# Hybrid attention block on one core: where the inverse softmax sums are turned, where the values are taken, and how many choice portions a step holds

## The reference, cut to what matters

```
h    = rms_norm(x, g_in);  proj = h @ w_in        # q, k, v, gate, indexer columns
oA   = dilated-window attention, 8 heads          # pairs "A": bias table per head
oB   = attention of 4 heads over the 256 keys that an indexer scores highest
oM   = cross attention of 4 heads into 256 memory tokens
o    = concat(oA, oB, oM) * silu(gate)
out  = rms_norm(x + o @ w_out, g_final)
```

## Time and profile before

| | |
|---|---|
| median of 3 runs | 714.0 us (713.66 to 715.45) |
| the profiled execution's own time | 713.12 us |
| its span | 711.3 us |
| PE busy | 673.2 us (95%) |
| DVE busy | 421.2 us (59%) |
| ACT busy | 333.4 us (47%) |
| POOL busy | 143.4 us (20%) |
| mean granted clock of PE | 0.994 |
| steps 8 to 15 (pair 1) | 187.8 to 260.9 us |
| steps 16 to 23 (pair 2) | 260.9 to 334.4 us |
| steps 24 to 31 (pair 3) | 334.4 to 409.1 us |

### The profile page before, as it was taken

One profiled execution on the slowest core, in us unless ns is written; L12 is line 12 of the kernel. 1 busy time (PEld: TensorE's weight loads), 2 busy tenths in 40 slices (PEclk: granted clock), 3 DMA queues, 4 the chain that ended last, 5 costly groups with the idle time before them and its releaser, 6 DMA issues.

```text
span 711.3 us, 11577 instructions
## 1 busy us (share of the span) xinstructions
PE 673.2 (95%) x4281; PEld 537.5 (76%) x4281; DVE 421.2 (59%) x991; ACT 333.4 (47%) x632; POOL 143.4 (20%) x95
## 2 busy tenths in 40 slices
PE   5999999999999999999999999989999999999993
PEld 4788887777778777787777777877888777777772
DVE  4857874396788576975797685652343354122247
ACT  6876653343335342644255434653563585122223
POOL 2021110111323013113114114210111166212101
PEclk9999999999999999999999999999999999999997
DMA  8521120111311121112111311101111416410005
GB/s 296 165 60 30 30 78 13 29 30 46 89 45 34 43 90 45 29 47 89 45 31 45 88 47 31 45 2 45 45 30 43 152 53 239 158 34 23 0 30 207
DMA packets 51863, 47.71 MB, mean 67 GB/s; under 512 B 5712, under 2 KB 44640, under 8 KB 51808
## 3 DMA queue, kind: packets, MB, share of 16 engines
q1 hardware_dynamic: 51808, 46.97, 21.6%
HBM read 39.62 MB, written 7.34 MB: 66 GB/s over the span
## 4 chain that ended last, share of the span: by engine, by line
PE 81%; DVE 10%; issue 3%; ACT 3%; DMA 2%; DVEq 0%; SPq 0%; ACTq 0%
PE j_ps L1471 27%; PE s_ps L1471 9%; PE o_ps L1630 8%; PE pt_ps L1604 7%; PE s_ps L1533 6%; PE s_ps L1680 5%; PE j_ps L1680 4%; PE o_ps L1471 4%; PE s_ps L1553 3%; DVE unread L1221 2%; PE pt_ps L1553 2%; PE s_ps L1686 1%; PE pt_ps L1652 1%; PE o_ps L1447 1%; PE j_ps L1447 1%
## 5 line engine op out<-in xcount | busy, mean ns | idle before, releaser
L1471 PE MATMUL j_ps<-h_hi,w_hl 128*128 128x512 f32 (+2 forms) x656 | 213.2, 391 | 4.7 <-DVE h_lo L1080 2.8
L1471 PEld LDWEIGHTS j_ps<-h_hi,w_hl 128*128 128x128 f32 (+1 forms) x656 | 121.1, 186 | 30.5 <-issue 4.9
L713 POOL TENSOR_TENSOR w_hl<-w_raw,w_hl 128x1024 fp32r<-128x1024 f32 (+1 forms) x29 | 68.2, 2350 | 322.7 <-ACT w_hl L815 311.4
L1471 PE MATMUL j_ps<-h_lo,w_hl 128*128 128x512 f32 (+2 forms) x328 | 125.4, 382 | 0.0
L998 ACT ACTIVATE prob<-prob,nmax 128x256 f32<-128x256 f32 (+7 forms) x128 | 89.9, 704 | 68.8 <-DVE nmax L1294 56.8
L986 ACT ACTIVATE probT<-pt_ps 128x512 f32<-128x512 f32 (+3 forms) x88 | 41.2, 468 | 124.3 <-PE pt_ps L1604 123.8
L1604 PE MATMUL pt_ps<-ident,prob 128*128 128x128 f32 x496 | 72.9, 280 | 8.9 <-DVE gate L1321 4.5
L1471 PE MATMUL s_ps<-h_hi,w_hl 128*128 128x512 f32 x224 | 73.7, 397 | 0.9 <-ACT qk L859 0.9
L1604 PEld LDWEIGHTS pt_ps<-ident,prob 128*128 128x128 f32 x496 | 54.5, 140 | 25.9 <-issue 18.8
L1471 PEld LDWEIGHTS j_ps<-h_lo,w_hl 128*128 128x128 f32 (+1 forms) x328 | 61.1, 186 | 11.1
L1221 DVE TENSOR_SCALAR_CACHE_REDUCE unread<-idx,tk 128x384 uint8<-128x384 f32 (+5 forms) x72 | 67.8, 942 | 1.3
(11 more groups left out here) (246 smaller groups left out, 1062.3 us busy)
## 6 DMA issues: line engine op xcount, KB each, us to landing
w_raw<-in_w_in_dram SPq DMA_DIRECT2D x27, 512.0 KB, 4.0
idx<-in_x_dram SPq DMA_DIRECT2D x8, 512.0 KB, 6.0
bias<-in_a_tab_dram SPq DMA_DIRECT2D x8, 512.0 KB, 4.7
mixed_scratch<-gate SPq DMA_DIRECT2D x12, 256.0 KB, 2.3
bias<-in_x_dram SPq DMA_DIRECT2D x4, 512.0 KB, 6.6
probT<-in_w_mem_kv_dram SPq DMA_DIRECT2D x4, 512.0 KB, 6.7
bias<-in_w_out_dram SPq DMA_DIRECT2D x4, 512.0 KB, 4.4
out_dram<-idx SPq DMA_DIRECT2D x4, 512.0 KB, 3.3
```

What stands on the lines that cost most here:

```text
L713: pool.tensor_tensor(w_hl[:, w % 2, 1, :, 0:n], raw_of(w)[:, :, 0:n], w_hl[:, w % 2, 0, :, 0:n].bitcast(F32), ALU.subtract).then_inc(w_lo_ ...
L1471: last = pe.matmul(bank[0:n, at:], a[:, k, 0:n], c[:, k, HALF * b + at:HALF * b + HALF], start=(k == 0 and q == 0), stop=(k == KD - 1 and ...
```

## The change

It has three parts.

1. The inverse sums get a PSUM bank of their own, `sums_bank = s_ps[1][:, HALF:T]`. For the groups of pairs 0 to 5 they are turned and multiplied into the gate in the first two steps of the next pair: group (p, g) in step 8(p+1) + g. `turn_sums` stands right behind `scores` there, `even_out` behind the copies, and the inversion is made a step earlier. Group (6, 0) goes to step 57. Groups (6, 1), (7, 0) and (7, 1) are handled in the step that ends them (`AT_ONCE`: 56, 60, 64), with `turn_sums` ahead of (or between) the values. The stores to the scratch tensor and the copies for the output projection wait for `linv_used` as well. `turn_prob` and `turn_values` no longer wait for it; a wide step's scores do.
2. Outside `AT_ONCE` the product of gate and values (`take_values`) stands behind `choose_portions(s, 1)`, the last portions of its step.
3. `choice_room` of an A pair becomes (2,2) for i = 0 and (1,2) for i = 4. With it every later slot moves to an earlier step; the last tile is settled in step 32. Slots per step, before and after (n.k is slot k of tile n):

The diff, cut to its core:

```diff
-PART_AT = {STEPS - NT - 3: (NP - 2, 0), STEPS - NT: (NP - 2, 1), STEPS - 4: (NP - 1, 0), STEPS: (NP - 1, 1)}
+PART_AT = {STEPS - NT: (NP - 2, 1), STEPS - NT + 1: (NP - 2, 0), STEPS - 4: (NP - 1, 0), STEPS: (NP - 1, 1)}
+EVEN_AT = {NT * (p + 1) + g: (p, g) for p in range(NP - 2) for g in range(2)}
+EVEN_AT.update(PART_AT)
+AT_ONCE = [s for s, (p, g) in EVEN_AT.items() if s == NT * p + 4 * g + 4 and p >= NP - 2]
+def evened(p, g):
+    return EVENED.index((p, g)) + 1
@@ choice_room
-    return [(2, 1), (2, 2), (2, 2), (2, 2), (1, 1), (1, 1), (1, 1), (1, 1)][i]
+    return [(2, 2), (2, 2), (2, 2), (2, 2), (1, 2), (1, 1), (1, 1), (1, 1)][i]
@@ SP
+                sp.wait_ge(linv_used, evened(p, g))
                 sp.dma_start(mixed_dram[p][:, cut], gates(p)[:, cut]).then_inc(og_stored[g], 16)
-                if s >= 1 and i % 4 == 0 and s <= (NP - 2) * NT:
-                    store_mixed((s - 1) // NT, (s - 1) % NT // 4)
+                if s in EVEN_AT and EVEN_AT[s][0] < NP - 2:
+                    store_mixed(*EVEN_AT[s])
@@ DVE
             def invert_sums(p, g):
                 for a in range(2):
                     dve.wait_ge(prob_ready[a], p * NT + 4 * g + 4)
+                if evened(p, g) > 1:
+                    dve.wait_ge(linv_turned, evened(p, g) - 1)
...
+            def even_out(p, g):
+                dve.wait_ge(linv_turned, evened(p, g))
+                dve.tensor_tensor(gates(p)[:, cut], sums_bank, gates(p)[:, cut], ALU.mult).then_inc(linv_used, 1)
+            def take_values(p, g):
+                dve.wait_ge(pv_done, CHUNK0[p * NT + 4 * g + 4])
+                dve.tensor_tensor(gates(p)[:, cut], o_ps[:, :], gates(p)[:, cut], ALU.mult).then_inc(og_ready, 1)
@@ DVE's loop
+                if s == STEPS:
+                    invert_sums(*EVEN_AT[s])
                 if s >= 1:
                     copy_probT(s - 1, 0)
...
-                if s >= 1 and (s - 1) % 4 == 3:
-                    invert_sums(pair_of_step(s - 1)[0], (s - 1) % NT // 4)
+                if s < STEPS and s in AT_ONCE:
+                    invert_sums(*EVEN_AT[s])
                 choose_portions(s, 0)
...
+                if s in EVEN_AT and s not in AT_ONCE:
+                    even_out(*EVEN_AT[s])
+                if s + 1 in EVEN_AT and s + 1 not in AT_ONCE:
+                    invert_sums(*EVEN_AT[s + 1])
...
-                if s >= 1 and (s - 1) % 4 == 3:
-                    finish_group(pair_of_step(s - 1)[0], (s - 1) % NT // 4)
+                if s in AT_ONCE:
+                    even_out(p, g)
+                    take_values(p, g)
...
                 choose_portions(s, 1)
+                if s >= 1 and s % 4 == 0 and s not in AT_ONCE:
+                    take_values(p, g)
@@ PE
-                    if a == 0 and s // 4 >= 1:
-                        pe.wait_ge(linv_used, s // 4)
...
+            def turn_sums(p, g):
+                pe.wait_ge(linv_ready, evened(p, g))
+                if evened(p, g) > 1:
+                    pe.wait_ge(linv_used, evened(p, g) - 1)
                 for c in range(4):
+                    last = pe.transpose(sums_bank[:, P * c:P * c + P], ..., ident[:, :])
@@ PE's loop
                     scores(s)
+                if s in EVEN_AT and s not in AT_ONCE:
+                    turn_sums(*EVEN_AT[s])
                 if s >= 1:
                     turn_prob(s - 1, 0)
...
-                if s >= 1:
+                if s >= 1 and two:
+                    values(s - 1, 0)
+                if s in AT_ONCE:
+                    turn_sums(*EVEN_AT[s])
+                if s >= 1 and not two:
                     values(s - 1, 0)
...
-                if s >= 1 and (s - 1) % 4 == 3:
-                    turn_sums(s - 1)
```

More of the change, by code:

```diff
@@ L184 @@
           STEPS - 5: [4], STEPS - 4: [5], STEPS - 3: [6], STEPS - 2: [7]}
-PART_AT = {STEPS - NT - 3: (NP - 2, 0), STEPS - NT: (NP - 2, 1), STEPS - 4: (NP - 1, 0), STEPS: (NP - 1, 1)}
+PART_AT = {STEPS - NT: (NP - 2, 1), STEPS - NT + 1: (NP - 2, 0), STEPS - 4: (NP - 1, 0), STEPS: (NP - 1, 1)}
 PARTS = list(PART_AT.values())
 PART_SLOT = {NP - 2: 6, NP - 1: 4}
+EVEN_AT = {NT * (p + 1) + g: (p, g) for p in range(NP - 2) for g in range(2)}
+EVEN_AT.update(PART_AT)
+EVENED = list(EVEN_AT.values())
+AT_ONCE = [s for s, (p, g) in EVEN_AT.items() if s == NT * p + 4 * g + 4 and p >= NP - 2]
+def evened(p, g):
+    return EVENED.index((p, g)) + 1
 def unit_number(t, b):
@@ L394, in build_program @@
         j_ps = ctx.enter_context(nc.psum_tensor("j_ps", [P, HALF], F32))
+        sums_bank = s_ps[1][:, HALF:T]
         turn_banks = [s_ps[0][:, 0:HALF], s_ps[0][:, HALF:T], s_ps[1][:, 0:HALF], s_ps[1][:, HALF:T],
@@ L1029, in _ @@
                     y_root(0, 0, len(EARLY_ROWS))
-                if s in PART_AT and s <= STEPS - NT:
+                if s in PART_AT and s <= STEPS - NT + 1:
                     part_hi(s)
@@ L1035, in _ @@
                     mix_hi(n)
-                if s in PART_AT and s > STEPS - NT:
+                if s in PART_AT and s > STEPS - NT + 1:
                     part_hi(s)
@@ L1303, in copy_probT @@
                 dve.tensor_copy(probT[:, g % 2, 1, 0:n, :], pt_ps[1][:, 0:n, :]).then_inc(pt_ready[1], 1)
-            groups = [0]
             def invert_sums(p, g):
@@ L1313, in invert_sums, with await_gate @@
                 dve.tensor_copy(linv[:, :, :, :], inverse.unsqueeze(3).broadcast_to([P, 4, 2, DH])).then_inc(linv_ready, 1)
-                groups[0] += 1
-            def finish_group(p, g):
+            def await_gate(p):
                 dve.wait_ge(gate_ready, sum(w <= W_OF["gate", p] for (what, _), w in W_OF.items() if what == "gate"))
-                dve.wait_ge(linv_turned, groups[0])
+            def even_out(p, g):
                 cut = slice(HALF * g, HALF * g + HALF)
-                dve.tensor_tensor(gates(p)[:, cut], pt_ps[0][:, :, :].rearrange("p a b -> p (a b)"),
-                                  gates(p)[:, cut], ALU.mult).then_inc(linv_used, 1)
-                dve.wait_ge(linv_used, groups[0])
+                dve.wait_ge(linv_turned, evened(p, g))
+                dve.tensor_tensor(gates(p)[:, cut], sums_bank, gates(p)[:, cut], ALU.mult).then_inc(linv_used, 1)
+            def take_values(p, g):
+                cut = slice(HALF * g, HALF * g + HALF)
                 dve.wait_ge(pv_done, CHUNK0[p * NT + 4 * g + 4])
@@ L1577, in scores @@
                     wait_evacuated(pe, lent[-1])
+                    if any(q < s for q in EVEN_AT):
+                        pe.wait_ge(linv_used, sum(q < s for q in EVEN_AT))
                 if s == 0:
@@ L1644, in turn_values @@
                 last.then_inc(v_turned, 1)
-            def turn_sums(s):
-                p, i = pair_of_step(s)
-                pe.wait_ge(linv_ready, s // 4 + 1)
-                pe.wait_ge(pt_ready[0], CHUNK0[s + 1])
+            def turn_sums(p, g):
+                pe.wait_ge(linv_ready, evened(p, g))
+                if evened(p, g) > 1:
+                    pe.wait_ge(linv_used, evened(p, g) - 1)
                 for c in range(4):
-                    last = pe.transpose(pt_ps[0][:, c, :], linv[:, c, :, :].rearrange("p a f -> p (a f)"), ident[:, :])
+                    last = pe.transpose(sums_bank[:, P * c:P * c + P], linv[:, c, :, :].rearrange("p a f -> p (a f)"),
+                                        ident[:, :])
                 last.then_inc(linv_turned, 1)
```

15 lines of the change are left out of this document (10 added, 5 removed).

## The result

The changed kernel took 714.88 us (median of 20 runs, 712.9 to 718.1), the kernel before 713.96 (20 runs, 712.49 to 715.45). The ratio is 1.0020, with a 95% interval of 1.0011 to 1.0028: 1.4 us slower, within 0.3% but on the other side of the forecast. The profiled execution took 716.13 us (span 714.3), 3.0 more than that of before.

What follows compares the result with a forecast made beforehand. TensorE was taken as the bound, busy 673.2 of 711.3 us, with DVE able to be late for it. Gains of 7.6 less losses of 6.8 made it 0.8 us faster, 713.2 against 714.0; range 711.5 to 715.0.

Steps and rivals of the forecast that it cites:

- The waits taken away: PE's 8 waits of `turn_prob` for DVE's gate multiplication (L1321) go, a gain of 4.5 us.
- rival C: The change does not decouple: `turn_sums` waits for the inverse in steps 17, 25 and 33; 716 at most, chance 0.05.
- Steps 15 and 34: Portions move to earlier steps: gain 0.9 us in step 15 and 1.1 us in step 34.
- Steps 18 and 19, 23, 27 and 28, 31: Extra or moved portions make DVE late: losses of 0.4, 0.4, 0.85 and 1.0 us.
- Step 29: Step 28 has 3 portions for 1; DVE's copy comes 3.65 us later against a margin of 1.25: loss 2.55 us.
- rival A: The portions fit: lateness 0.5 us too large everywhere, step 29 costs 1 us; 709.8 us, chance 0.33.
- For steps 8, 16, ... the inverse was made a step before and costs nothing: No wait of `turn_sums` in these steps; one of 1.6 us in step 9, its inverse being behind two portions.
- Step 41: The turn of (4,1) fills a hole before the values: 0.8 us gained beyond the 0.4 of the wait removed.
- Step 56: The turn of sums stands between two groups of values: gain 0.3 us.
- The turns of sums at their new place: The 16 turns, some 0.6 us each, only change place, which is nothing for PE where its queue is full.
- The sign for DVE's wait: If the forecast is right, DVE's wait at L1321 falls from 33.7 us to a few.
- Rival B: DVE becomes the bound in steps 27 to 31, 0.4 us later at each of nine places; 716.8 us, chance 0.17.

Runs made afterwards that it cites:

- rooms_old: The change without its third part: sums' bank and late values kept, portions as in the kernel before; 710.89 us, 0.9954 to the kernel before.
- invert_early: The change with the inversion of the sums moved ahead of the portions of place 0; 712.54 us, 0.9973 to the kernel before.
- copy_form: The change with the copy that spreads the inverse written as an accumulating multiplication by 1 and minimum; 714.86 us, 0.9998 to the kernel before.
- front_rooms_old: The change with the old portions, and with inversion and multiplication of the sums both ahead of the portions; 0.9886 to the kernel before.
- rooms_only: The kernel before with the third part alone, one more portion at i = 0 and i = 4; 721.06 us, 1.0106 to the kernel before.

## Why the prediction was wrong

The forecast was 713.2 us, 0.8 faster; it came out 0.9 slower by the medians and 1.4 by the ratio. In short: the sum had no term for the clock, had a wait of step 9 in step 8, and missed the copy of step 40 that GpSimd blocks. Most of its other terms held, so part of the small total error is luck: errors of both signs cancel in it. By its own steps:

- **The waits taken away: right.** The 4.5 us of L1321 are gone (rival C is out: no `turn_sums` waits in steps 17, 25 and 33).
- **Steps 15 and 34: right.** -1.05 and -1.19 us, for 0.9 and 1.1.
- **Steps 18 and 19, 23, 27 and 28, 31: near.** +0.61 in sum for 0.4; +0.45 for 0.4; +0.69 and, against the -0.59 of `rooms_old`, +0.41 for 0.85; +0.87 for 1.0. The slot of L1247 at 1024 keys met POOL's operation in step 31, as said, and took 2.41 us, where the earlier trace rows had 2.01 at 640 keys:

```profile
402.88 2.38 POOL L726 TENSOR_TENSOR w_hl<-w_raw,w_hl 128x1024 fp32r<-128x1024 f32 x1 [22.11 <-ACT w_hl L828]
...
403.93 2.41 DVE L1247 SCALAR_TENSOR_TENSOR picked<-picked,idx 128x1024 f32<-128x1024 f32 x1
```

- **Step 29: right as a wait, wrong as a cost.** The wait is 2.22 us for the 2.55 forecast, in the place named (from a margin put at 1.25 us, where the earlier trace rows give 1.15). Without the slow clock the step is 1.79 us longer, with it 3.37. This rules out rival A, which needed a wait of 1 us there.

```profile
376.82 1.31 PE L1566 MATMUL s_ps<-qk 64*128 64x512 f32 x12
...
383.42 0.69 DVE L1317 COPY probT<-pt_ps 128x512 f32<-128x512 f32 x1
...
384.25 0.30 PE L1637 MATMUL pt_ps<-ident,prob 128*128 128x128 f32 x1 [2.22 <-DVE probT L1317]
```

- **The portions as a whole: right but for the clock.** The terms of part 3 come to a loss of 5.2 - 2.0 = 3.2 us. From `rooms_old` to the change the named steps grow by 4.8 us in sum, of which the stretch behind step 29 is 1.6, so 3.2.

- **"For steps 8, 16, ... the inverse was made a step before and costs nothing": wrong.** Step 7 is 7.5 us long and the inverse stands behind its portions, so `turn_sums` waits 1.94 us in step 8; step 9 has no wait then. I had put 1.6 us in step 9, so the size was near and the place was wrong. The cause, an inversion behind portions, is shown by `invert_early` (step 8 from +3.48 to -0.16).
- **Step 41: wrong by some 2 us.** I gave the turn of (4,1) a hole and 1.2 us of gain. The copy ahead of it was stretched from 0.43 to 2.00 us by POOL's operation, `turn_sums` waited 1.00 us and the step was 0.83 us longer. I had named this very lock, for L1233 alone, and not asked which other instruction of DVE would move beside POOL. `copy_form` (-0.73) and `front_rooms_old` (-0.73) show the step without it.
- **Step 56: wrong, small.** A gain of 0.1 us for 0.3.
- **The step that failed most: no term for the clock.** The sum takes a wait at its own length. Here three waits were each followed by 3.4 us at half clock, which cost 1.6, 1.6 and 1.5 us in the profile, and by the clocks of the timed runs some 2.5 us on the mean, more than the whole loss. With the waits filled the change is 0.18% faster than before (1.3 us, interval 0.5 to 2.1), near the 0.8 forecast. Of before no row ahead of the tail showed such a stretch, so its price was not to be read there; the granted clock of the earlier trace rows was 1.00. That a wait of 2 us could bring a slow clock of its own I did not ask.
- **The turns of sums at their new place: better than put.** With 0.6 us for a turn that arrives and 0.4 for a wait that goes, steps 16 and 17 should together grow by 0.2 us; they shrink by 0.21, and steps 24 and 25, 32 and 33 do the same. No run takes this apart. It and step 41 are the two errors that cancel.
- **The sign for DVE's wait: not met.** "Down from 33.7 us to a few" came out as 12.1.

Rival B (DVE becomes the bound in steps 27 to 31, 716.8) named the right place and came near the profiled time, but not by its mechanism: the copies of steps 27 and 31 were no later than I had counted, and its mark was badly set: "more than nine steps with over 9 us" is nearly met by PE's eleven waits of 10.1 us after, but also by the 17 of 10.5 in the earlier trace rows. Half of the 10.1 is in steps 8, 29 and 41. In the profile the waits alone leave a gain of 1.7 us; only with the clock's 4.7 us is it a loss of 3.0. `rooms_only` is what rival B looks like: 16 places, 12.6 us, 1.1% slower. Two prices of rivals don't follow from their own terms: A's losses come to 2.6 us and not 3.4 (709.0 us), and C's, 0.4 and 1 us in three steps, to 717.4 us and not 716.

## What to carry to other kernels

A wait of 1 to 2 us on TensorE cost 1.5 to 1.6 us beside its own length in the executions where the clock fell behind it. Slices of 18 us hide that; compare the mean granted clock of the runs (here 0.987 against 0.994), look at windows as short as the stretch, and try harmless turns in a wait that can't be removed. Compare two profiles only after checking that they had the same clock. When DVE's order is changed, list every plain copy that will now start while GpSimd works, and price it by the longest such overlap in the trace. When work goes to a bank of its own, move everything that fills and frees that bank ahead of the work that can wait (here the portions), not only the part that is waited for now: here that is worth 0.7% with the old portions (0.9954 to 0.9886) and 0.8% with the new (1.0020 to 0.9943).

## What the runs showed of the hardware that I had not expected

- The half-clock stretches were 3.4 us long each in every kernel that had them ahead of the tail, and did not come in each execution of the same kernel: after step 8 in the profile of the change and not in its repetition, at the same wait of 1.94 us and with PE busy for the same 1.46 of 3.40 us ahead of it. So how idle PE was does not decide it alone; what does stays open.
- The accumulating form of the spreading copy took 0.69 us with and without POOL beside it, the plain copy 0.43 alone and up to 2.43 beside it.
